# Activation rows 288 floats apart and weight slots on multiples of 256 bytes in a three-block transformer kernel

## The chip, the cores and the metric

The kernel is one launch on one NeuronCore of a Trainium2 chip. The metric is the device time of one execution in microseconds, median of the runs. All arithmetic is float32; the results are [1, 256, 1024] float32.

## What is computed

Three layers on 256 tokens of width 1024. The first two carry 16 meta tokens as well, 272 in all.

```python
def swiglu(x, w_gate, w_up, w_down):
    return (jax.nn.silu(x @ w_gate) * (x @ w_up)) @ w_down

h = concat(meta_tokens, x)                       # 272 tokens
for i in range(2):
    h = h + 0.5 * rmsnorm(swiglu(rmsnorm(h, g0), ...), g1)     # d_ff 2816
    m = neighborhood_attention(...) if i == 0 else diff_attention(...)
    h = h + rmsnorm(m, g3)
    h = h + 0.5 * rmsnorm(swiglu(rmsnorm(h, g4), ...), g5)
x = h[16:]                                       # 256 tokens
x = x + rms_norm(mix(rms_norm(x)) @ w_out, g)    # block attention and mLSTM
x = x + rms_norm(square(relu(rms_norm(x) @ w_up)) @ w_down, g) # width 4096
```

From the last attention's output on (sub-layer 4), only the 256 tokens are carried.

## The kernel before, in words

The work is eight sub-layers (`SUBS`, numbered k = 0 to 7): four FFNs (0, 2, 3, 5), three mixers (NA = 1, DA = 4, MIX = 6) and the last MLP (7). Each has two phases (`PHASES[2k]`, `PHASES[2k+1]`): a product from the normalised input x, and a product from the hidden or attended activations back to the residual h. Activations are held transposed, features on the 128 partitions and tokens along a row: `x_hi[:, k, :]` is chunk k of 8, one row per partition.

**Three products.** Each float32 operand is split in a high and a low part of type float32r. `product` (lines 645 to 648) issues `w_hi` x `x_hi` (L646), `w_hi` x `x_lo` (L647) and `w_lo` x `x_hi` (L648) for one chunk k and one half m of a panel; `chunk` does both halves, so one row k of the activations is read by six matmuls in a row: hi, lo, hi, hi, lo, hi. The weights are the stationary operand (128 x 128 floats), the activations the moving one, with 272 or 256 columns. `shared_chunk` (L709, L715) does the same for the first two panels of a sub-layer together, 96 matmuls in each of eight openings; `opening_panel` (L733) is the very first panel, 48 matmuls. `row_products` (L874 to L876), in the last phase, swaps the operands: `mlp_hi`/`mlp_lo` are stationary and 512 columns of `w_hi`/`w_lo` move.

**Panels.** A panel is 256 output columns by up to 1024 rows of weights, 8192 bytes a partition. SP loads it into one of four slots of `raw` (L534) in pieces of 1024 bytes, ScalarE rounds it to `w_hi` (L1400), VectorE subtracts to `w_lo` (L1856), in place over `raw`. A chunk takes 1024 bytes of a slot, its half m 512.

**Second phase of an FFN.** VectorE draws gate and up from the accumulators (`z`, L1999), ScalarE applies silu, VectorE multiplies (L2663), ScalarE rounds to `hid_hi` (L1828) and VectorE writes the rest to `hid_lo` (L2666), two of the 22 rows at a time. `down` then reads `hid_hi[:, k, :]` and `hid_lo[:, k, :]` as moving rows.

**Order.** Each engine runs a program written out by hand, tied by semaphores; no planner decides it.

**Addresses.** A program-wide cursor places all buffers in SBUF by hand (`sb`), every one on a multiple of 64 bytes. `region` and what follows is used in turn by the sub-layers. The first free byte is 16481, and so the buffers of this change start here (bytes in a partition; row k is 272 x 4 = 1088 bytes on, 64 modulo 256):

| buffer | start | modulo 256 | rows start, modulo 256 |
|---|---|---|---|
| w_lo (and raw) | 16512 | 128 | every chunk and half 128 |
| w_hi | 49280 | 128 | every chunk and half 128 |
| x_hi | 90752 | 128 | 128, 192, 0, 64, and again |
| x_lo | 99456 | 128 | the same |
| hid_hi | 140608 | 64 | 64, 128, 192, 0 |
| hid_lo | 164544 | 192 | 192, 0, 64, 128 |
| mlp_hi, mlp_lo | 140608, 173376 | 64 | all 64 (rows of 1024 bytes) |

Of the kernel before, what the change touches and what calls it, by code (L numbers as in the profile page):

```python
# [22 lines left out]
F32 = mybir.dt.float32  # L23
# [7 lines left out]
NM = 16  # L31
NT = NX + NM
FF = 2816
FC = FF // P
# [101 lines left out]
def program(nc, A, out):  # L136

    with ExitStack() as ctx:
# [3 lines left out]

        start = (nc.sbuf_base + 63) // 64 * 64
        cursor = [start]
# [12 lines left out]
        x_hi_at = cursor[0]  # L157
        x_hi = sb("x_hi", [P, DC, NT], F32R)
        x_lo_at = cursor[0]
        x_lo = sb("x_lo", [P, DC, NT], F32R)  # L160
        y_at = cursor[0]
# [22 lines left out]
        root = sb("root", [P, 4, 8])  # L184
        region = cursor[0]
        bias_at = region + 2 * FC * NT * 4
        end = bias_at + 32 * NT * 4
# [3 lines left out]
        c = [region]  # L191
        hid_hi = sb("hid_hi", [P, FC, NT], F32R, c)
        hid_lo = sb("hid_lo", [P, FC, NT], F32R, c)

# [40 lines left out]
        assert c[0] <= z_at  # L235
        c = [end]
        line = sb("line", [8, 2 * NT - 1 - NM], F32, c)
        assert c[0] <= nc.sbuf_usable_end

# [232 lines left out]
        def out_bank(k, g):  # L472

            return acc[:, :, g % 2, :] if k == NA else acc[:, g % 2, :, :]
# [169 lines left out]
        def _(pe):  # L644
# [75 lines left out]
            def opening_panel():  # L720

                for part, xs, ready in ((w_hi, x_hi, x_hi_ready), (w_hi, x_lo, x_ready), (w_lo, x_hi, None)):
                    if part is w_lo:
                        pe.wait_ge(w_lo_ready, 1)
                    for k in range(DC):
                        if ready is not None:
                            pe.wait_ge(ready, k + 1)
                        if ready is x_hi_ready and k == 0:
                            keep_warm(aux[:, 3, :], 12)
                            pe.wait_ge(w_hi_ready, 1)  # L730
                        for m in range(2):
                            w = slice(k * CW + m * P, k * CW + m * P + P)
                            mm = nc.tensor.matmul(acc[:, 0, m, 0:NT], part[:, 0, w], xs[:, k, :],  # L733
                                                  start=ready is x_hi_ready and k == 0,
                                                  stop=part is w_lo and k == DC - 1)
                mm.then_inc(panel_used, 1)
# [83 lines left out]
            def from_na_heads():  # L820
# [6 lines left out]
                for c in range(8):  # L827
                    if c in (2, 3):
                        na_turn(2 * c)
                        na_turn(2 * c + 1)  # L830
                    pe.wait_ge(x_ready, SPLIT_HEADS[NA] + c + 1)
                    mm = chunk(out_bank(NA, 0)[:, :, 0:NT], slot, c, x_hi, x_lo, c, c == 0, c == 7)
                mm.then_inc(panel_used, 1)
# [554 lines left out]
        def _(act):  # L1388
# [343 lines left out]
            for k in range(8):  # L1732
# [3 lines left out]
                if k in (NA, DA, MIX):  # L1736
# [32 lines left out]
                    if k == NA:  # L1769
# [6 lines left out]
                        for c in range(8):  # L1776
                            if c == 2:
                                high(n, 2, 5)
                            act.wait_ge(s["o_turned"], c + 1)
                            nc.scalar.activation(x_hi[:, c, :], na_banks[c][:, 0:NT], ACT.Copy).then_inc(x_hi_ready, 1)  # L1780
                        act.wait_ge(lam_step, 2)
# [64 lines left out]
        def _(dve):  # L1846
# [598 lines left out]
            for k in range(8):  # L2445
# [3 lines left out]
                if k in (NA, DA, MIX):  # L2449
# [50 lines left out]
                    if k == NA:  # L2500
# [41 lines left out]
                        for c in range(8):  # L2542
                            if c == 4:
                                evict_rows(k, 8)
                            if c in (0, 4):
                                dve.wait_ge(meta_gathered, 28 + c)
                            dve.wait_ge(x_hi_ready, SPLIT_HEADS[k] + c + 1)
                            nc.vector.tensor_tensor(x_lo[:, c, :], na_banks[c][:, 0:NT], x_hi[:, c, :].bitcast(F32),
                                                    ALU.subtract).then_inc(x_ready, 1)
# [268 lines left out]
```

## Time and profile before

| | |
|---|---|
| median of 3 runs | 1434.66 us (1434.41 to 1439.29) |
| profiled execution, span from first to last instruction | 1436.0 us |
| PE (TensorE matmul) busy | 1419.0 us, 99%, 10988 matmuls |
| DVE (VectorE) busy | 947.8 us, 66% |
| ACT (ScalarE) busy | 662.0 us, 46% |
| POOL (GpSimd) busy | 45.6 us, 3% |
| chain that ended last | PE 92%, DVE 3%, ACT 2%, DMA 2% |
| granted TensorE clock, mean | 0.998 |

The times of the runs are those of whole executions; the profiled execution's own time is known by its span only, and that is 1.3 us over the median. Matmuls overlap, so a matmul's duration in the rows (0.28 us) is not what it costs: cost is the distance from its start to the next one's. A stretch of the trace with n matmuls in it gives that distance as its length over n.

### The profile page before, as it was taken

To read this page: it belongs to the slowest core of one execution; us is meant where nothing else is said; L and a number is where in the kernel's file an instruction comes from. 1 tells how busy PE (TensorE), PEld (TensorE's weight loads), DVE (VectorE), ACT (ScalarE), POOL (GpSimd) and SP (SyncE) were. 2 spreads that over 40 slices of the span, in tenths; PEclk is the share of its full clock that TensorE was granted. 3 is DMA by queue.
4 is the path that set the end of the run, shared out by engine and by line. 5 is a ranking of instruction groups with operands and counts; after the bars stand their busy time and mean duration, and the time that the engine had idled before them with its cause. 6 is when DMAs were issued, how large, how long until landed. Compare 5 with 4: busy or idle time off the path is not lost.

```text
span 1436.0 us, 26258 instructions
## 1 busy us (share of the span) xinstructions
PE 1419.0 (99%) x10988; PEld 1361.9 (95%) x10988; DVE 947.8 (66%) x1223; ACT 662.0 (46%) x876; POOL 45.6 (3%) x72
## 2 busy tenths in 40 slices
PE   9999999999999999999999999999999999999998
PEld 9999999978999999999999988999999997999887
DVE  6656568566865555866557677876656975787653
ACT  5444345544544343544435357544444555544432
POOL 0000010010000000000001000000001010000000
PEclk9999999999999999999999999999999999999999
DMA  7586765511455576455454640465656540356552
GB/s 219 177 226 186 206 195 161 176 61 60 147 176 175 173 217 200 147 176 175 145 168 157 205 147 2 146 206 176 191 175 205 172 152 30 119 176 208 187 195 99
DMA packets 238904, 233.99 MB, mean 163 GB/s; under 512 B 29791, under 2 KB 233492, under 8 KB 238816
## 3 DMA queue, kind: packets, MB, share of 16 engines
q1 hardware_dynamic: 238024, 232.33, 52.4%
q8 instruction: 66, 1.08, 0.3%
q10 hardware_dynamic: 792, 0.40, 0.1%
q14 instruction: 22, 0.18, 0.0%
HBM read 231.52 MB, written 1.12 MB: 162 GB/s over the span
## 4 chain that ended last, share of the span: by engine, by line
PE 92%; DVE 3%; ACT 2%; DMA 2%; issue 1%; DVEq 0%; SPq 0%; ACTq 0%
PE acc L646 22%; PE acc L647 22%; PE acc L648 22%; PE acc L709 4%; PE aux L876 2%; PE aux L875 2%; PE aux L874 2%; PE acc L715 2%; PE aux L646 2%; PE aux L647 2%; PE aux L648 2%; PE aux L941 1%; PE acc L1154 1%; ACT w_hi L1400 1%; PE acc L1262 1%
## 5 line engine op out<-in xcount | busy, mean ns | idle before, releaser
L646 PE MATMUL acc<-x_hi,w_hi 128*128 128x272 f32 (+1 forms) x1960 | 559.8, 286 | 1.6 <-DVE z L1999 0.9
L647 PE MATMUL acc<-x_lo,w_hi 128*128 128x272 f32 (+1 forms) x1960 | 559.6, 286 | 0.0
L1856 DVE TENSOR_TENSOR w_lo<-raw,w_hi 128x2048 fp32r<-128x2048 f32 (+1 forms) x229 | 482.0, 2109 | 117.3 <-ACT w_hi L1400 116.6
L648 PE MATMUL acc<-x_hi,w_lo 128*128 128x272 f32 (+1 forms) x1960 | 557.9, 285 | 0.0
L1400 ACT ACTIVATE w_hi<-raw 128x2048 fp32r<-128x2048 f32 (+3 forms) x251 | 407.0, 1627 | 171.1 <-DMA raw<-in_ffn_w_down 52.7
L646 PEld LDWEIGHTS acc<-x_hi,w_hi 128*128 128x128 f32 x1960 | 369.4, 188 | 4.5 <-issue 1.7
L647 PEld LDWEIGHTS acc<-x_lo,w_hi 128*128 128x128 f32 x1960 | 368.2, 188 | 0.3 <-issue 0.2
L648 PEld LDWEIGHTS acc<-x_hi,w_lo 128*128 128x128 f32 x1960 | 368.3, 188 | 0.0
L646 PE MATMUL acc<-hid_hi,w_hi 128*128 128x272 f32 (+1 forms) x704 | 201.9, 287 | 0.0
L647 PE MATMUL acc<-hid_lo,w_hi 128*128 128x272 f32 (+1 forms) x704 | 201.6, 286 | 0.0
L648 PE MATMUL acc<-hid_hi,w_lo 128*128 128x272 f32 (+1 forms) x704 | 200.7, 285 | 0.0
L1999 DVE TENSOR_TENSOR z<-acc,rstd 128x544 f32<-128x544 f32 (+1 forms) x95 | 67.2, 712 | 136.0 <-PE acc L648 135.8
L1828 ACT ACTIVATE hid_hi<-z 128x544 f32 (+3 forms) x44 | 28.7, 652 | 248.5 <-DVE z L2663 246.4
L648 PEld LDWEIGHTS acc<-hid_hi,w_lo 128*128 128x128 f32 x704 | 132.6, 188 | 0.0
L647 PEld LDWEIGHTS acc<-hid_lo,w_hi 128*128 128x128 f32 x704 | 132.6, 188 | 0.0
L646 PEld LDWEIGHTS acc<-hid_hi,w_hi 128*128 128x128 f32 x704 | 132.4, 188 | 0.1
L709 PE MATMUL acc<-x_hi,w_hi 128*128 128x272 f32 (+1 forms) x256 | 66.2, 289 | 4.7 <-ACT x_hi L1463 4.7
L709 PE MATMUL acc<-x_hi,w_lo 128*128 128x272 f32 (+1 forms) x256 | 64.9, 284 | 0.0
L646 PE MATMUL aux<-x_hi,w_hi 128*128 128x272 f32 (+1 forms) x200 | 59.0, 295 | 1.9 <-DVE w_lo L1856 1.9
L2666 DVE TENSOR_TENSOR hid_lo<-z,hid_hi 128x544 f32 (+3 forms) x44 | 31.6, 718 | 40.3 <-ACT hid_hi L1828 40.3
L647 PE MATMUL aux<-x_lo,w_hi 128*128 128x272 f32 (+1 forms) x200 | 57.7, 288 | 0.0
L648 PE MATMUL aux<-x_hi,w_lo 128*128 128x272 f32 (+1 forms) x200 | 57.6, 288 | 0.0
(340 smaller groups left out, 1610.5 us busy)
## 6 DMA issues: line engine op xcount, KB each, us to landing
raw<-in_ffn_w_gate SPq DMA_DIRECT2D x44, 1024.0 KB, 5.4
raw<-in_ffn_w_up SPq DMA_DIRECT2D x44, 1024.0 KB, 5.4
raw<-in_ffn_w_down SPq DMA_DIRECT2D x32, 768.0 KB, 4.9
raw<-in_ffn_w_down SPq DMA_DIRECT2D x32, 640.0 KB, 4.4
raw<-in_w_up SPq DMA_DIRECT2D x16, 1024.0 KB, 5.4
raw<-in_w_down SPq DMA_DIRECT2D x16, 1024.0 KB, 4.8
raw<-in_na_w_qkv SPq DMA_DIRECT2D x12, 1024.0 KB, 5.2
raw<-in_da_w_qkv SPq DMA_DIRECT2D x12, 1024.0 KB, 5.3
```

The source lines that it names most:

```text
L646: nc.tensor.matmul(o, wh, xh, start=first, stop=False)
L647: nc.tensor.matmul(o, wh, xl, start=False, stop=False)
L648: return nc.tensor.matmul(o, wl, xh, start=False, stop=last)
L709: nc.tensor.matmul(banks(n, 0, j)[:, m, 0:tokens], part[:, (ph.p0 + j) % SLOTS, w], x_hi[:, k, 0:tokens], start=k == 0 and part is w_hi, s ...
L715: mm = nc.tensor.matmul(banks(n, 0, j)[:, m, 0:tokens], w_hi[:, (ph.p0 + j) % SLOTS, w], x_lo[:, k, 0:tokens], start=False, stop=k == DC - 1)
L874: nc.tensor.matmul(o, mlp_hi[:, k, tok], w_hi[:, slot, w], start=first, stop=False)
L875: nc.tensor.matmul(o, mlp_hi[:, k, tok], w_lo[:, slot, w], start=False, stop=False)
L876: return nc.tensor.matmul(o, mlp_lo[:, k, tok], w_hi[:, slot, w], start=False, stop=last)
L1400: ins = nc.scalar.activation(w_hi[:, slot, w], raw[:, slot, w], ACT.Copy)
L1856: nc.vector.tensor_tensor(w_lo[:, slot, w], raw[:, slot, w], w_hi[:, slot, w].bitcast(F32), ALU.subtract)\
L1999: ins = nc.vector.tensor_tensor(dst, src, spread(0, tokens), ALU.mult)
L2666: nc.vector.tensor_tensor(hid_lo[:, dst, 0:tokens], up, hid_hi[:, dst, 0:tokens].bitcast(F32), ALU.subtract).then_inc(hid_ready, 1)
```

## The change

Constants and addresses. A new `STRIDE = 288` replaces 272 as the row length of `x_hi`, `x_lo`, `hid_hi` and `hid_lo`; the 16 floats at a row's end are not used, and the code that took whole rows now takes `0:NT`. A row is 1152 bytes, 128 modulo 256. The cursor starts at a multiple of 256 bytes, and so does `region`. The constant `line`, which had its own place at the end, moves to `y_at`. The buffers then start at 16640 (w_lo), 49408 (w_hi), 90880 (x_hi), 100096 (x_lo), 141824 (hid_hi), 167168 (hid_lo), 141824 and 174592 (mlp_hi, mlp_lo), all 0 modulo 256; the rows of x and hid start at 0 and 128 modulo 256 in turn, the weight chunks and the mlp rows all at 0. Buffers behind them move along.

No instruction is added, removed or moved on any engine, and no wait changes. Only the form of those that write `hid_hi` and `hid_lo` is another: two rows of 272 (2 x 272) where there were 544 floats in one piece.

```diff
--- before.py
+++ after.py
@@ -30,6 +30,7 @@
 NX = 256
 NM = 16
 NT = NX + NM
+STRIDE = 288
 FF = 2816
 FC = FF // P
 FF2 = 4096
@@ -140,7 +141,7 @@
             return ctx.enter_context(nc.semaphore(name))
 
 
-        start = (nc.sbuf_base + 63) // 64 * 64
+        start = (nc.sbuf_base + 255) // 256 * 256
         cursor = [start]
 
         def sb(name, shape, dt=F32, at=None):
@@ -155,9 +156,9 @@
         w_hi = sb("w_hi", [P, SLOTS, FULL * CW], F32R)
         h = sb("h", [P, DC, NT])
         x_hi_at = cursor[0]
-        x_hi = sb("x_hi", [P, DC, NT], F32R)
+        x_hi = sb("x_hi", [P, DC, STRIDE], F32R)
         x_lo_at = cursor[0]
-        x_lo = sb("x_lo", [P, DC, NT], F32R)
+        x_lo = sb("x_lo", [P, DC, STRIDE], F32R)
         y_at = cursor[0]
         y = sb("y", [P, DC, NT])
         z = sb("z", [P, 2, 2, 2, NT])
@@ -182,15 +183,15 @@
         stat = sb("stat", [P, 4, 16])
         na_mask = sb("na_mask", [P, GRID_W])
         root = sb("root", [P, 4, 8])
-        region = cursor[0]
-        bias_at = region + 2 * FC * NT * 4
+        region = (cursor[0] + 255) // 256 * 256
+        bias_at = region + 2 * FC * STRIDE * 4
         end = bias_at + 32 * NT * 4
         assert end <= nc.sbuf_usable_end, (end, nc.sbuf_usable_end)
 
 
         c = [region]
-        hid_hi = sb("hid_hi", [P, FC, NT], F32R, c)
-        hid_lo = sb("hid_lo", [P, FC, NT], F32R, c)
+        hid_hi = sb("hid_hi", [P, FC, STRIDE], F32R, c)
+        hid_lo = sb("hid_lo", [P, FC, STRIDE], F32R, c)
 
         c = [region]
         mlp_hi = sb("mlp_hi", [P, FF2 // P, NX], F32R, c)
@@ -233,9 +234,8 @@
         meta_in = sb("meta_in", [16, NM], F32, c)
         bands = sb("bands", [16, BANDS], F32, c)
         assert c[0] <= z_at
-        c = [end]
+        c = [y_at]
         line = sb("line", [8, 2 * NT - 1 - NM], F32, c)
-        assert c[0] <= nc.sbuf_usable_end
 
         c = [region]
         proj = sb("proj", [P, 24, NT], F32, c)
@@ -730,7 +730,7 @@
                             pe.wait_ge(w_hi_ready, 1)
                         for m in range(2):
                             w = slice(k * CW + m * P, k * CW + m * P + P)
-                            mm = nc.tensor.matmul(acc[:, 0, m, 0:NT], part[:, 0, w], xs[:, k, :],
+                            mm = nc.tensor.matmul(acc[:, 0, m, 0:NT], part[:, 0, w], xs[:, k, 0:NT],
                                                   start=ready is x_hi_ready and k == 0,
                                                   stop=part is w_lo and k == DC - 1)
                 mm.then_inc(panel_used, 1)
@@ -829,7 +829,8 @@
                         na_turn(2 * c)
                         na_turn(2 * c + 1)
                     pe.wait_ge(x_ready, SPLIT_HEADS[NA] + c + 1)
-                    mm = chunk(out_bank(NA, 0)[:, :, 0:NT], slot, c, x_hi, x_lo, c, c == 0, c == 7)
+                    mm = chunk(out_bank(NA, 0)[:, :, 0:NT], slot, c, x_hi[:, :, 0:NT], x_lo[:, :, 0:NT], c,
+                               c == 0, c == 7)
                 mm.then_inc(panel_used, 1)
                 for j in (1, 2):
                     panel(n, 0, j, ph.a0 + j - 1, out_bank(NA, j), range(8), True, True, x_hi[:, :, 0:NT], x_lo[:, :, 0:NT],
@@ -1777,7 +1778,7 @@
                             if c == 2:
                                 high(n, 2, 5)
                             act.wait_ge(s["o_turned"], c + 1)
-                            nc.scalar.activation(x_hi[:, c, :], na_banks[c][:, 0:NT], ACT.Copy).then_inc(x_hi_ready, 1)
+                            nc.scalar.activation(x_hi[:, c, 0:NT], na_banks[c][:, 0:NT], ACT.Copy).then_inc(x_hi_ready, 1)
                         act.wait_ge(lam_step, 2)
                         nc.scalar.activation(lam[:, 2:4], lam[:, 0:2], ACT.Exp).then_inc(lam_exp, 1)
                     if k == DA:
@@ -2545,7 +2546,7 @@
                             if c in (0, 4):
                                 dve.wait_ge(meta_gathered, 28 + c)
                             dve.wait_ge(x_hi_ready, SPLIT_HEADS[k] + c + 1)
-                            nc.vector.tensor_tensor(x_lo[:, c, :], na_banks[c][:, 0:NT], x_hi[:, c, :].bitcast(F32),
+                            nc.vector.tensor_tensor(x_lo[:, c, 0:NT], na_banks[c][:, 0:NT], x_hi[:, c, 0:NT].bitcast(F32),
                                                     ALU.subtract).then_inc(x_ready, 1)
 
                         dve.wait_ge(lam_exp, 1)
```

## Rows read from the trace of the kernel before

**Rows 1.** Five stretches: length, busy us (count) per engine PE to POOL, clock, DMA.

```profile
395.00:495.00 100.00, 100.00 (x802) 100.00 (x801) 60.99 (x51) 41.78 (x35) 0.00 (x0) 1.00 0.57 177
505.00:560.00 55.00, 55.00 (x442) 55.00 (x441) 30.95 (x26) 22.34 (x20) 4.64 (x3) 1.00 0.69 201
...
945.00:1040.00 95.00, 95.00 (x815) 95.00 (x814) 61.58 (x53) 42.73 (x36) 0.00 (x0) 1.00 0.58 180
1045.00:1095.00 50.00, 50.00 (x425) 50.00 (x424) 28.91 (x27) 21.98 (x20) 5.65 (x6) 1.00 0.58 184
...
1345.00:1420.00 75.00, 75.00 (x329) 61.56 (x328) 36.98 (x21) 27.33 (x16) 0.00 (x0) 1.00 0.50 175
```

**Rows 2.** Groups by shape, PE: line, names, shape, count, busy us, mean ns.

```profile
L647 PE MATMUL acc<-x_lo,w_hi 128*128 128x272 f32 x1248 | 360.9, 289 | 0.0
...
L646 PE MATMUL acc<-x_hi,w_hi 128*128 128x256 f32 x712 | 200.7, 282 | 1.5 <-DVE z L1999 0.9 <-DVE x_lo L2189 0.6
...
L646 PE MATMUL acc<-hid_hi,w_hi 128*128 128x272 f32 x528 | 152.3, 288 | 0.0
...
L646 PE MATMUL acc<-hid_hi,w_hi 128*128 128x256 f32 x176 | 49.6, 282 | 0.0
...
L646 PE MATMUL aux<-x_hi,w_hi 128*128 128x272 f32 x112 | 32.9, 294 | 0.0
...
L646 PE MATMUL aux<-x_hi,w_hi 128*128 128x256 f32 x88 | 26.1, 297 | 1.9 <-DVE w_lo L1856 1.9
```

**Rows 3.** Timeline of PE, first matmul of rows k = 4 to 7 and 0, 272 columns.

```profile
604.51 0.28 PE L646 MATMUL acc<-x_hi,w_hi 128*128 128x272 f32 x1
...
605.27 0.28 PE L646 MATMUL acc<-x_hi,w_hi 128*128 128x272 f32 x1
...
606.02 0.29 PE L646 MATMUL acc<-x_hi,w_hi 128*128 128x272 f32 x1
...
606.77 0.28 PE L646 MATMUL acc<-x_hi,w_hi 128*128 128x272 f32 x1
...
607.51 0.28 PE L646 MATMUL acc<-x_hi,w_hi 128*128 128x272 f32 x1
```

**Rows 4.** Timeline of PE, the same five places in a half panel with 256 columns.

```profile
972.58 0.28 PE L646 MATMUL acc<-x_hi,w_hi 128*128 128x256 f32 x1
...
973.29 0.28 PE L646 MATMUL acc<-x_hi,w_hi 128*128 128x256 f32 x1
...
974.00 0.28 PE L646 MATMUL acc<-x_hi,w_hi 128*128 128x256 f32 x1
...
974.70 0.28 PE L646 MATMUL acc<-x_hi,w_hi 128*128 128x256 f32 x1
...
975.39 0.28 PE L646 MATMUL acc<-x_hi,w_hi 128*128 128x256 f32 x1
```

**Rows 5.** Timeline of PE, first matmul of rows 8, 9 and 10 of hid, 256 columns.

```profile
1048.44 0.28 PE L646 MATMUL acc<-hid_hi,w_hi 128*128 128x256 f32 x1
...
1049.14 0.29 PE L646 MATMUL acc<-hid_hi,w_hi 128*128 128x256 f32 x1
...
1049.86 0.28 PE L646 MATMUL acc<-hid_hi,w_hi 128*128 128x256 f32 x1
```

**Rows 6.** Timeline of PE, runs of matmuls whose weight load sets the distance.

```profile
217.12 1.95 PE L941 MATMUL aux<-ones 128*128 128x128 f32 x16
...
334.04 1.90 PE L1154 MATMUL acc<-v_rows,turned_pair 128*128 128x64 f32 x16
```

**Rows 7.** Groups by shape, DVE: eviction of z and writing of hid_lo.

```profile
L1999 DVE TENSOR_TENSOR z<-acc,rstd 128x544 f32<-128x544 f32 x61 | 43.9, 724 | 103.4 <-PE acc L648 103.3
...
L2666 DVE TENSOR_TENSOR hid_lo<-z,hid_hi 128x544 f32 x24 | 17.4, 726 | 22.9 <-ACT hid_hi L1828 22.9
```

**Rows 8.** Waits of PE; chain of waits: start us, us, what.

```profile
PE acc L709 <- ACT x_hi L1463: 4.7, 7, 1.3
...
559.88 7.11 DMA raw<-in_ffn_w_up
```

## The prediction, made before the changed kernel ran

> **What bounds the kernel now.** I read the busy time of every engine in five long stretches first, then the instruction groups by shape, then the timeline of TensorE inside single panels, and last the waits and the chain of waits. In the five stretches [rows 1] TensorE is busy the whole time (100.00 of 100.00 us), at the full granted clock (1.00, its 2.4 GHz level), while VectorE has 61 and ScalarE 42 us of work in 100. So inside a phase nothing but the spacing of the matmuls counts. The spacing comes from the counts: 802 matmuls touch the stretch 395 to 495, about 2 of them begun before it, so 100 us / 800 = 125.0 ns for one with 272 columns of x. In the same way 505 to 560 gives 125.1 (272 columns of hid), 945 to 1040 gives 116.9 (256, x), 1045 to 1095 gives 118.3 (256, hid) and 1345 to 1420 gives 229.1 (512 columns).
>
> How many there are: the shapes [rows 2] show one of the three lines of a product, so each count stands three times. 272 columns of x: 3 x (1248 + 112) = 4080, and 48 of the opening panel and 384 of the shared openings (eight openings of 96 matmuls, four of them with 272 columns): 4512. 272 of hid: 3 x 528 = 1584. 256 of x: 3 x (712 + 88) + 384 = 2784. 256 of hid: 3 x 176 = 528. With the spacings above that is 564 + 198 + 325 + 62 = 1149 us of a span of 1436.0; 384 matmuls of 512 columns add 88. A nanosecond on each of the 9408 is 9.4 us, or 0.66%, and that is the lever of this change.
>
> **Does the address of a row show in the trace?** It does. All weight chunks start at 128 modulo 256 bytes; rows of x start at 128, 192, 0, 64 in turn. In one half panel of 272 columns [rows 3] the four blocks of six matmuls, one block for each row k, take 0.76, 0.75, 0.75 and 0.74 us. With 256 columns [rows 4] they take 0.71, 0.71, 0.70 and 0.69 us. Such half panels repeat, in steps of 3.00 and 2.81 us, through the whole phase. In hid with 256 columns [rows 5] the block of row 8 (hi at 64, lo at 192) takes 0.70 us and that of row 9 (hi at 128, lo at 0) 0.72 us. Three times the same sign: rows on a multiple of 128 bytes are not the cheap ones. They average (0.76 + 0.75) / 12 = 125.8 ns against 124.2 with 272 columns, (0.71 + 0.70) / 12 = 117.5 against 116.7 with 256.
>
> **Part by part.**
> Moving rows, 288 floats apart. Rows now start at 0 and 128 in turn, in x and in hid, so only two of the four classes are left, and both stand in the trace before. 272 columns of x: 125.8 is read from starts with 10 ns steps, a nanosecond is its error, and against 125.0 it is +0.8; the neighbouring reading, all four blocks alike, is 0; I take +0.6, nearer to the one that shows a difference: 4512 x 0.6 ns = +2.7 us. 272 of hid: to the same 125.6 from 125.1, 1584 x 0.5 = +0.8 us. 256 of x: 117.5 against the mean of rows 4, 2.81 / 24 = 117.1, 2784 x 0.4 = +1.1 us. 256 of hid: today hi and lo lie 128 bytes apart in phase, and afterwards they are alike as in x, so from 118.3 to 117.5: 528 x -0.8 = -0.4 us. Sum +4.2 us.
>
> Weights at 0 modulo 256 instead of 128. No row shows the slots elsewhere. The nearest are matmuls with few columns, whose spacing is that of their weight load: sixteen with the stationary tile ones (at 192) span 1.95 us, sixteen with v_rows (at 64) 1.90 us [rows 6]; less the last one's own 0.28, and over fifteen, that is 0.11 for both. The start of the load makes no difference there, so I take 0 for it alone. Its phase relative to the moving row is another matter: rows of x lie at 0, 64, 128, 192 beyond the weights now and at 0 and 128 afterwards, which are the same two blocks that I used. Phase by itself and phase against the weights give the same sum; only an effect of both together would break it. Bounds for moving rows and weights as one: every block like the cheapest (0.74 / 6 = 123.3 and 0.69 / 6 = 115.0) is -1.7 x 6096 - 2.1 x 2784 - 3.3 x 528 = -18.0 us; every block like the dearest (0.76 / 6 = 126.7, 0.72 / 6 = 120.0) is +1.7 x 6096 + 2.9 x 2784 + 1.7 x 528 = +19.3 us. Farther down lies the price of a column in the 512-column matmuls, 229.1 / 512 = 0.447 ns, where starts count half as much: 121.7 and 114.5 ns, -29 us. The 384 matmuls of 512 columns move too (0 instead of 128 under w, 0 instead of 64 under the stationary mlp tiles): at most 2 ns each either way, 0.8 us, taken as 0.
>
> The Trainium skill (SBUF — State Buffer, section on the DMA port swizzle) says that SBUF is read in 16-byte lines, and by that alone all four classes would cost the same and the change would do nothing. Rows 3 to 5 do not agree: 0.69 and 0.71 us for the same six shapes. The skill (TensorE: Matmul & The Clock Gate, Part 2) also says that loading the next weights takes no read bandwidth from the running matmul; by that rule the phase between the two is nothing, and the sum stays at the 4.2 us from the rows alone.
>
> VectorE and ScalarE forms. The 44 pairs that write hid go from 544 contiguous floats to 2 x 272. hid_lo takes 726 ns today; the eviction of z from two accumulator banks, whose source is already in two pieces, takes 724 [rows 7]. Nothing to pay, and both engines have a third of the time free [rows 1]: if it cost 50 ns, it would hide under a panel of 6 us. The order of instructions and all waits are unchanged on every engine, SP's queue included. The table line lies over onehot, which the matmul that precedes it has read: nothing.
>
> DMA. Weights now land on multiples of 256. The longest transfer on the chain takes 7.11 us ahead of a sub-layer's opening; TensorE waits there for x_hi, 4.7 us over seven openings [rows 8]. Those 4.7 us bound any gain; a loss has no reason. I take 0, since the chain passes VectorE and ScalarE work after the landing. The skill (DMA: Bandwidth & Descriptors, How a descriptor splits into AXI transactions) lets each of our 1 KB pieces fall from 36 beats to 32, if it holds for the writing side, which no row here shows.
>
> **Sum.** 1434.7 + 4.2 = 1438.9 us. The sum was made on the profiled execution, whose span of 1436.0 is 1.3 us above the median of the runs, 1434.7; I add it to the median.
>
> **Rivals.**
> Faster: with both operands on multiples of 128 the stalls vanish, as they nearly do today in the block at 64 (0.69 us). For it: 125.0 and 116.9 ns both lie above columns alone (272 at 0.447 = 121.7, 256 at 0.447 = 114.5), the excess varies with the address, and hid with mixed phases is dearer than x (118.3 against 116.9). Against it: the blocks at 0 and 128 are the slow ones. All blocks at the cheapest: 1434.7 - 18.0 = 1417.
> Slower: moving row and weights start on the same phase in even rows and collide. Even rows pay the dearest block (126.7 and 120.0), odd rows stay at today's mean. +0.85 x 6096 + 1.45 x 2784 + 0.1 x 528 = +9.3 us: 1444. It decides from 0.8 ns a matmul (7.2 us) on. For it: the block at 128, in phase with its weights, is the longest of rows 3. Against: in rows 4 the one at 192 is as long.
> No effect: the block differences come from what stands before a matmul and average out in any layout: 1434.7. Here too if the phase matters within 64 bytes only, since every start stays a multiple of 64.
>
> **Chances.** Forecast 0.36, no effect 0.12, faster rival 0.30, slower rival 0.22. A measurement of this kernel can tell about 0.5% (7.2 us) from no change. Of the forecast's case 0.01 falls to faster and 0.04 to slower, so faster 0.31, same 0.43, slower 0.26. The range reaches from 1414, past the cheapest blocks, to 1447, past the slower rival, and leaves out about 0.2: the 29 us case and the dearest blocks everywhere.
>
> **What would show it.** Right: matmul counts in stretches of the same phase and length of about 798 instead of 802 (100 us, 272 columns of x), about 812 instead of 815 (95 us, 256 of x), about 428 instead of 425 (50 us, 256 of hid); blocks of two kinds only, taking turns. Wrong: a spacing under 124 or 116 ns, or over 126.5; a change of wait times at the openings by more than 2 us; hid_lo over 800 ns.

## The result, and the profile after

| | median | range | runs |
|---|---|---|---|
| before | 1437.14 us | 1434.41 to 1439.72 | 6 |
| changed | 1442.89 us | 1441.04 to 1444.94 | 6 |

The ratio is 1.0044, interval 1.0025 to 1.0062. The change costs 5.75 us by the medians and 6.1 us by the profiled spans (1442.1 against 1436.0). That is a small, real loss, and under the 0.5% that the prediction set as its bound for "slower". In some executions of either kernel the granted clock falls to its 1.2 GHz level for a few microseconds and the runs of one kernel lie some 5 us apart, so it helps to compare those with a mean clock of 1.000: 1434.4 to 1435.2 us for the kernel before (four of 17 in the last series below), 1441.0 and 1442.8 for the changed one.

Line numbers behind L800 are one higher in the changed kernel. These are its five stretches, answering to [rows 1] (columns as there; each kind of stretch begins some microseconds later than before):

```profile
395.00:495.00 100.00, 100.00 (x797) 99.90 (x796) 60.97 (x53) 41.82 (x35) 0.00 (x0) 1.00 0.55 171
505.00:560.00 55.00, 55.00 (x440) 55.00 (x440) 31.41 (x28) 21.88 (x20) 4.63 (x3) 1.00 0.69 196
945.00:1040.00 95.00, 95.00 (x805) 95.00 (x804) 60.15 (x51) 41.52 (x35) 0.00 (x0) 1.00 0.59 185
1050.00:1100.00 50.00, 50.00 (x425) 50.00 (x424) 29.61 (x26) 21.35 (x19) 7.27 (x8) 1.00 0.59 180
1352.00:1427.00 75.00, 75.00 (x333) 62.12 (x332) 36.93 (x21) 27.34 (x16) 0.00 (x0) 1.00 0.51 174
```

TensorE is still busy throughout at full clock, so again the counts are the spacing. They are 797 for 802 (272 columns of x), 440 for 442 (272 of hid), 805 for 815 (256 of x), 425 for 425 (256 of hid) and 333 for 329 (512 columns). Three kinds got slower, one stayed, one got faster. The prediction's signs were 798, 812 and 428 for x with 272 and 256 columns and hid with 256: the first came true, the other two did not.

For finer numbers I took the distance from the start of one matmul to the start of the one hundreds later, inside one long phase, divided by their number (816 or 552 matmuls of x, 498 of hid). "First" is the opening FFN, "later" are the two others with 272 columns. All values in ns:

| | before | after |
|---|---|---|
| 272, x, first / later | 125.0 / 125.0 | 126.1 / 125.6 |
| 272, hid, first / later | 125.5 / 125.1 | 126.3 / 125.6 |
| 256, x | 116.9 | 118.3 |
| 256, hid | 118.4 | 118.3 |
| 512 | 229.1 | 227.0 |

The timeline of TensorE in the changed kernel, 272 columns, first matmul of five successive rows k (start us, duration us; answers to [rows 3]):

```profile
613.10 0.29 PE L646 MATMUL acc<-x_hi,w_hi 128*128 128x272 f32 x1
...
613.85 0.29 PE L646 MATMUL acc<-x_hi,w_hi 128*128 128x272 f32 x1
...
614.61 0.29 PE L646 MATMUL acc<-x_hi,w_hi 128*128 128x272 f32 x1
...
615.36 0.29 PE L646 MATMUL acc<-x_hi,w_hi 128*128 128x272 f32 x1
...
616.12 0.29 PE L646 MATMUL acc<-x_hi,w_hi 128*128 128x272 f32 x1
```

The blocks take 0.75, 0.76, 0.75 and 0.76 us (748, 759, 747 and 759 ns by the starts in the trace): two kinds taking turns, as forecast. Those in phase with the weights are the cheaper ones. The same with 256 columns, answering to [rows 4]:

```profile
949.50 0.28 PE L646 MATMUL acc<-x_hi,w_hi 128*128 128x256 f32 x1
...
950.22 0.28 PE L646 MATMUL acc<-x_hi,w_hi 128*128 128x256 f32 x1
...
950.93 0.28 PE L646 MATMUL acc<-x_hi,w_hi 128*128 128x256 f32 x1
...
951.64 0.28 PE L646 MATMUL acc<-x_hi,w_hi 128*128 128x256 f32 x1
...
952.35 0.28 PE L646 MATMUL acc<-x_hi,w_hi 128*128 128x256 f32 x1
```

0.72, 0.71, 0.71 and 0.71 us (713, 712, 707 and 708 ns), where the prediction took 0.705 (117.5 x 6). Here the two kinds do not take turns: rows k = 0 and 2 both start in phase with the weights, and are 6 ns apart. The two blocks at 0 and 128 cost more in this company than they did among the four.

**Where the 6.1 us lie.** Both kernels issue the same 10988 matmuls in the same order, so the start of matmul number n in one trace less that in the other shows where time is gained or lost. Over the three long phases with 272 columns of x: +0.9, +0.5 and +0.5 us. Over the three with 272 of hid: +0.4, +0.2, +0.2. Over the two long ones with 256 of x: +1.1 and +0.8. 256 of hid: 0.0. 512 columns: -0.8. That is +3.8 us from spacing. The first 150 matmuls give +1.0. Both kernels start 6 to 7 matmuls per microsecond at first and 11 later; the step comes before 5 us in the kernel before and before 7 us in the changed one, and the clock column, 1.00 throughout, does not tell why. The experiments scatter there from 0.0 to +1.2, and one and the same kernel (starts only, profiled twice) has +0.8 and 0.0, so no layout is charged with it. The mixer of sub-layer 6 gives +3.1, that of sub-layer 4 -1.1; what is left, the openings, the first mixer and short pieces, gives -0.7. The +3.1 is mostly a stretch at the lower clock that the profiled execution of before did not have. Windows of the changed kernel:

```profile
1200.00:1205.00 5.00, 4.55 (x30) 3.63 (x28) 3.12 (x11) 2.46 (x12) 0.00 (x0) 1.00 0.00 0
1205.00:1212.00 7.00, 7.00 (x25) 5.36 (x23) 3.85 (x10) 2.18 (x8) 0.00 (x0) 0.51 0.00 0
```

and of the kernel before:

```profile
900.00:906.00 6.00, 5.07 (x30) 5.07 (x31) 4.65 (x6) 3.53 (x3) 1.91 (x1) 0.72 0.98 319
1205.00:1212.00 7.00, 6.96 (x44) 5.32 (x44) 3.58 (x13) 4.25 (x19) 0.00 (x0) 1.00 0.01 2
```

The clock column is 0.51 there (1.2 GHz) against 1.00 (2.4 GHz), while TensorE had been busy 4.55 of the 5 us ahead of it. The profile before has such a piece in sub-layer 4's mixer instead (0.72 over 900 to 906), the changed kernel has none there. Such pieces come and go between executions (of the two profiles of starts only, one has such a piece of 3.4 us and the other none) and are no part of the change's own cost.

Little else moved. The wait lists of TensorE name L709 for x_hi with 4.5 us over seven openings (4.7 in [rows 8]). VectorE's groups by shape, answering to [rows 7]:

```profile
L2000 DVE TENSOR_TENSOR z<-acc,rstd 128x544 f32<-128x544 f32 x61 | 43.9, 724 | 105.4 <-PE acc L648 105.3
L2667 DVE TENSOR_TENSOR hid_lo<-z,hid_hi 128x544 f32 x24 | 17.4, 726 | 22.9 <-ACT hid_hi L1829 22.9
```

hid_lo in two pieces of 272 takes the same 726 ns as in one of 544. The long transfer of the chain, answering to the 7.11 us of [rows 8]:

```profile
563.26 6.37 DMA raw<-in_ffn_w_up
```

It takes 0.7 us less, and the stretch ahead of the opening of sub-layer 3, which waits for it, shrinks from 5.9 to 5.2 us. The weights' start is not the reason: in the two profiles of starts only (below), with weights at 0, the stretch takes 5.9 and 6.3 us, and in the layout with weights at 128 and x at 0 it takes 5.0. It has 5.9 us or more in every profile with rows of x 272 floats apart, and 5.2 or less in every one with longer rows. Why is open.

### The profile page after: what moved, and what is told of

Read it like the earlier page. It is cut to its first block, busy times and chain, and to the rows that moved or that the text cites. A ratio compares the mean times of both kernels' runs of the same rounds, so it can differ in the third digit from the quotient of the medians.

```text
span 1442.1 us, 26258 instructions
## 1 busy us (share of the span) xinstructions
PE 1426.3 (99%) x10988; PEld 1370.1 (95%) x10988; DVE 947.4 (66%) x1223; ACT 661.7 (46%) x876; POOL 45.5 (3%) x72
## 4 chain that ended last, share of the span: by engine, by line
PE 93%; DVE 3%; ACT 2%; DMA 1%; issue 1%; DVEq 0%; SPq 0%; ACTq 0%
PE acc L646 22%; PE acc L647 22%; PE acc L648 22%; PE acc L709 4%; PE aux L877 2%; PE aux L875 2%; PE aux L876 2%; PE acc L715 2%; PE aux L646 2%; PE aux L647 2%; PE aux L648 2%; PE aux L942 1%; PE acc L1155 1%; ACT w_hi L1401 1%; PE acc L1263 1%
## 5 line engine op out<-in xcount | busy, mean ns | idle before, releaser
L709 PE MATMUL acc<-x_hi,w_hi 128*128 128x272 f32 (+1 forms) x256 | 66.6, 290 | 4.5 <-ACT x_hi L1464 4.5
L709 PE MATMUL acc<-x_hi,w_lo 128*128 128x272 f32 (+1 forms) x256 | 65.2, 285 | 0.0
```

The lines of the kernel that those rows point to most:

```text
L709: nc.tensor.matmul(banks(n, 0, j)[:, m, 0:tokens], part[:, (ph.p0 + j) % SLOTS, w], x_hi[:, k, 0:tokens], start=k == 0 and part is w_hi, s ...
```

## Experiments

**Theory.** The spacing is set by where the moving row starts relative to the stationary tile, modulo 256 bytes ("beyond the weights"), not by the row's own address. **Rivals:** the row's own address counts; or only the mixture of phases counts; or one of the two parts of the change (rows apart, buffers' start) carries the whole loss. In the first four expectations, theory P is the distance, theory M the row's own address, rival T a cost of the row length or of a changing phase.

All experiments write `X_ROW` and `HID_ROW` where the changed kernel has `STRIDE`. The first four give every row of x the same phase (320 floats, 1280 bytes, are a multiple of 256), leave hid at 272 floats and at its old distance from the weights, and place the weights and x. Diffs are against the changed kernel, and "..." stands for lines left out.

### All rows of x 192 bytes beyond the weights, two ways

```diff
-STRIDE = 288
+X_ROW = 320
+HID_ROW = 272
...
-        start = (nc.sbuf_base + 255) // 256 * 256
+        start = (nc.sbuf_base + 127) // 256 * 256 + 128
...
         h = sb("h", [P, DC, NT])
+        cursor[0] = (cursor[0] + 191) // 256 * 256 + 64
         x_hi_at = cursor[0]
...
-        region = (cursor[0] + 255) // 256 * 256
+        region = (cursor[0] + 191) // 256 * 256 + 64
```

> Rows of x 320 floats (1280 bytes, a multiple of 256) apart, so that all 16 rows start at 64 modulo 256, weights at 128 as before the change, hid as before (272 apart). Theory P (phase of the moving row against the weight chunk sets the spacing): the cheapest block of before for all rows, 115.3 ns with 256 columns and 123.6 ns with 272, so about -11 us on the span of before (1436). Theory M (the moving row's own phase, whatever the weights): the same here. Rival T (what costs is the change of phase from row to row, or the row stride itself): same spacing in all kernels with this stride. Rival N (blocks differ by accident): 125.0 and 117.0, as before.

The second has the same distance at another address: weights at 0, x and region at 192.

```diff
         start = (nc.sbuf_base + 255) // 256 * 256
...
+        cursor[0] = (cursor[0] + 63) // 256 * 256 + 192
         x_hi_at = cursor[0]
...
-        region = (cursor[0] + 255) // 256 * 256
+        region = (cursor[0] + 63) // 256 * 256 + 192
```

> The same, but everything moved: weights at 0, all rows of x at 192, so 192 beyond the weights as in one_phase_64, and hid in the same place relative to the weights. Theory P: spacings equal to one_phase_64 within 0.3 ns. Theory M: those of rows at 192 in before, 125.1 ns with 272 columns and 117.8 with 256, about 2 ns more than one_phase_64.

### All rows 128 beyond, and in phase

As the first, but with x at 0, `cursor[0] = (cursor[0] + 255) // 256 * 256`, and with x at 128, `cursor[0] = (cursor[0] + 127) // 256 * 256 + 128`. The weights are at 128 in both.

> All rows of x at 0, weights at 128 (128 apart). Theory P and M: the blocks of before at 0, 125.8 ns with 272 columns, 117.0 with 256; P says also 126.5 for 272 from the odd rows of the changed kernel, which stand 128 from their weights too. Rival T: equal to one_phase_64.

> All rows of x at 128, in phase with the weights. Theory P: between the blocks of before at 128 (125.4 and 117.9 ns) and the even rows of the changed kernel (125.0 and 118.2). Theory M: 126.5 with 272 columns, as the rows at 128 in the changed kernel. Rival T: equal to one_phase_64.

The four together: 1425.84, 1425.88, 1446.86 and 1453.8 us, one run each, against 1439.8 for the kernel before in the same series. Windows of the kernel before, 272 and 256 columns of x:

```profile
400.00:490.00 90.00, 90.00 (x722) 90.00 (x721) 54.03 (x45) 38.56 (x31) 0.00 (x0) 1.00 0.57 175
950.00:1030.00 80.00, 80.00 (x686) 80.00 (x685) 51.25 (x43) 35.89 (x29) 0.00 (x0) 1.00 0.61 191
```

x at 64, weights at 128 (the third row is in the last MLP, 256 columns too):

```profile
400.00:490.00 90.00, 90.00 (x732) 90.00 (x732) 55.65 (x46) 36.25 (x29) 0.00 (x0) 1.00 0.58 181
950.00:1030.00 80.00, 80.00 (x682) 80.00 (x681) 49.82 (x44) 34.83 (x29) 0.00 (x0) 1.00 0.59 182
1292.00:1322.00 30.00, 30.00 (x268) 30.00 (x266) 23.03 (x23) 13.24 (x11) 0.00 (x0) 1.00 0.66 209
```

x at 192, weights at 0:

```profile
400.00:490.00 90.00, 90.00 (x732) 90.00 (x731) 55.66 (x46) 36.60 (x30) 0.00 (x0) 1.00 0.58 180
950.00:1030.00 80.00, 80.00 (x708) 80.00 (x708) 50.75 (x44) 34.65 (x29) 0.00 (x0) 1.00 0.61 191
1292.00:1322.00 30.00, 30.00 (x257) 30.00 (x256) 22.60 (x22) 12.20 (x10) 0.00 (x0) 1.00 0.67 212
```

x at 0, weights at 128:

```profile
400.00:490.00 90.00, 90.00 (x713) 90.00 (x712) 55.09 (x47) 37.38 (x31) 0.00 (x0) 1.00 0.55 173
950.00:1030.00 80.00, 80.00 (x676) 80.00 (x675) 51.34 (x43) 34.06 (x28) 0.00 (x0) 1.00 0.58 181
```

x and weights both at 128; the first row is the opening FFN:

```profile
52.00:142.00 90.00, 90.00 (x713) 90.00 (x712) 53.44 (x45) 34.59 (x28) 0.00 (x0) 1.00 0.70 197
400.00:490.00 90.00, 90.00 (x721) 90.00 (x720) 54.74 (x47) 39.37 (x32) 0.00 (x0) 1.00 0.55 174
950.00:1030.00 80.00, 80.00 (x669) 80.00 (x669) 49.56 (x43) 34.70 (x29) 0.00 (x0) 1.00 0.58 184
```

With 272 columns, the two layouts at 192 beyond give the same 90 us / 730 = 123.3 ns, and 128 beyond gives 90 / 711 = 126.6. The one at 0 differs from the one at 64 in nothing but 64 bytes of start, and its three long phases with 272 columns take 8.0 us more; all 4512 matmuls at 3.3 ns would be 15 us, an estimate. In phase gives 126.6 in the first FFN and 125.2 later. Rival T is out, as four layouts of one row length differ. The distance holds as theory P has it, but P's numbers, read off the blocks of the mixture, often missed: 128 beyond with 256 columns took 118.7 and not 117.0, in phase took 120.0 and not 118. The last layout also sat at the lower clock for 20.5 us in the mixer of sub-layer 6, which cost it 9.5 us there, so its time of 1453.8 overstates it.

With 256 columns a second thing shows. The two layouts of the same distance take turns: 80 / 680 = 117.6 and 30 / 266 = 112.8 in one, 80 / 706 = 113.3 and 30 / 255 = 117.6 in the other. By starts over whole phases these are 117.78 and 113.33 ns in both. One distance has two steady spacings here, and what decides between them was not found. With 256 columns the distance thus fixes the spacing only up to this choice.

### The same row address, other weights

Weights at 128 and x at 192, 64 beyond.

```diff
-        start = (nc.sbuf_base + 255) // 256 * 256
+        start = (nc.sbuf_base + 127) // 256 * 256 + 128
...
+        cursor[0] = (cursor[0] + 63) // 256 * 256 + 192
         x_hi_at = cursor[0]
...
-        region = (cursor[0] + 255) // 256 * 256
+        region = (cursor[0] + 191) // 256 * 256 + 64
```

> All rows of x at 192, weights at 128: the phase that is missing, 64 beyond the weights (one_phase_192 had 192 beyond). Theory P: the settled part of before's blocks at 192, 117.5 with 256 columns, 125.1 with 272. If only odd multiples of 64 mattered, it would equal one_phase_64: 123.3.

1442.72 us (before: 1439.46 in this series). Windows:

```profile
400.00:490.00 90.00, 90.00 (x713) 90.00 (x712) 55.08 (x47) 37.69 (x32) 0.00 (x0) 1.00 0.55 171
950.00:1030.00 80.00, 80.00 (x708) 80.00 (x708) 54.02 (x47) 37.11 (x32) 0.00 (x0) 1.00 0.59 185
1292.00:1322.00 30.00, 30.00 (x257) 30.00 (x256) 22.67 (x22) 12.19 (x10) 0.00 (x0) 1.00 0.62 191
```

Rows of x at 192 as in the second experiment, but 713 matmuls in 90 us instead of 732: 126.6 for 123.3 ns. Here only the weights' start differs, and with it the phase between the two (and the start of region, which x's products with 272 columns do not touch). This is the comparison that decides against the rival of the row's own address. With 256 columns, 64 beyond has the same two spacings as 192 beyond, 113.3 and 117.8. Both numbers of the expectation, 125.1 and 117.5, missed: the row's price alone isn't that of its block in the mixture.

VectorE, ScalarE and the DMA queues write the weight slots, so their addresses moved with the weights too. Do they set the spacing? In the first experiment I sorted some 600 matmuls of sub-layer 2 (272 columns) by what ran beside them. They are 123.3 ns apart where VectorE works all the time (354) and where it pauses (206), 123.3 where ScalarE works (238) and where it pauses (330), and 123.3 where no DMA engine moves data (197). With x at 0 each of these groups has 126.7. So the 3.3 ns aren't a matter of the other engines; TensorE's own two streams, weights and moving rows, are left.

### The two parts of the change alone

Starts only: rows 272 floats apart as before, everything else as the changed kernel.

```diff
-STRIDE = 288
+X_ROW = 272
+HID_ROW = 272
```

> The second part of the change alone: weights, x_hi, x_lo and region start at 0 modulo 256, rows stay 272 floats apart. Theory P (phase of the moving row against the weight chunk): the rows of x stand 0, 64, 128, 192 from the weights as in before, in hid the four phases only begin elsewhere; spacings as in before within 0.2 ns (125.0 and 117.0, hid 125.1 and 118.4), span within 1 us of before's. Rival A (alignment of the weights to 256 counts by itself): another spacing everywhere.

Rows only: 288 floats apart, starts as before (weights and x at 128, region at 64).

```diff
-STRIDE = 288
+X_ROW = 288
+HID_ROW = 288
...
-        start = (nc.sbuf_base + 255) // 256 * 256
+        start = (nc.sbuf_base + 127) // 256 * 256 + 128
...
-        region = (cursor[0] + 255) // 256 * 256
+        region = (cursor[0] + 191) // 256 * 256 + 64
```

> The first part alone: rows of x and hid 288 floats apart, starts as in before (weights at 128, x at 128, region at 64). Theory P: x stands 0 and 128 from its weights in turn, as in the changed kernel: 125.6 and 118.3 ns. hid_hi and hid_lo stand at 192 and 64 from them: between one_phase_64's 123.3 and the unseen phase 64, so below 125.0 with 272 columns and below 118 with 256. Sum: 2 to 4 us under the changed kernel. Rival A: the loss comes with the starts, and this kernel is no slower than before in x.

Starts only took 1434.82 us, and was timed again in more rounds:

> starts_only again, timed: starts at 0 modulo 256, rows 272 apart. Theory P: ratio 0.9985 to 1.001 against before; only the last phase gains, 384 matmuls of 512 columns at 2.1 ns, 0.8 us. Rival A (the starts carry a part of the change's +5.7 us): 1.001 or more.

1436.71 us against 1437.93, ratio 0.9996, interval 0.9985 to 1.0007: the starts alone are worth nothing that can be measured. (The first profile's span, 1433.0 against 1436.0, is shorter than the 1 us of the expectation allows, for it has no stretch at the lower clock; the second has 1434.8.) Windows of starts only, 272 and 256 columns of x:

```profile
400.00:490.00 90.00, 90.00 (x722) 90.00 (x721) 54.11 (x45) 39.37 (x32) 0.00 (x0) 1.00 0.56 175
950.00:1030.00 80.00, 80.00 (x686) 80.00 (x686) 49.68 (x43) 34.36 (x29) 0.00 (x0) 1.00 0.61 189
...
1342.00:1417.00 75.00, 75.00 (x333) 62.10 (x332) 37.84 (x22) 27.37 (x16) 0.00 (x0) 1.00 0.52 179
```

The counts of the split matmuls are those of the kernel before, 722 and 686. Moving weights and rows of x together leaves every distance between them as it was, and every spacing with it, which is the theory once more. (hid meets the same four distances, begun at another one.) Only the 512 columns gain (333 for 329), all that the change had to offer.

Rows only took 1448.24 us (before: 1439.46):

```profile
400.00:490.00 90.00, 90.00 (x719) 90.00 (x719) 55.81 (x47) 39.12 (x32) 0.00 (x0) 1.00 0.55 173
950.00:1030.00 80.00, 80.00 (x679) 80.00 (x678) 51.23 (x43) 35.64 (x30) 0.00 (x0) 1.00 0.60 186
...
1050.00:1090.00 40.00, 40.00 (x347) 40.00 (x346) 22.93 (x20) 15.43 (x14) 1.30 (x1) 1.00 0.62 192
```

In x it has the whole loss: 126.11, 125.56 and 118.33 ns by starts, to the hundredth those of the changed kernel. Its hid, 64 and 192 beyond the weights in turn instead of 0 and 128, goes the other way, to 116.1 ns with 256 columns. The time of 1448.24 holds 20.5 us at the lower clock, in this profile:

```profile
1205.00:1212.00 7.00, 7.00 (x26) 5.58 (x25) 3.68 (x9) 2.44 (x11) 0.00 (x0) 0.50 0.01 2
1212.00:1225.00 13.00, 13.00 (x55) 10.09 (x54) 4.50 (x25) 5.22 (x21) 0.00 (x0) 0.60 0.00 0
```

That mixer is 8.9 us longer than before; the rest of the kernel only 1.5, of which 1.2 lie in the first 150 matmuls. By the times alone one would have charged all of it to the rows. The expected 2 to 4 us under the changed kernel therefore did not show in the span (1446.4 against 1442.1). Of its spacings, that of hid with 256 columns came as expected, and 272 columns of hid took 125.0, which is the mean of 123.3 and 126.7, the prices of 192 and 64 beyond alone.

### Distances of 32 bytes

Is it the multiple of 64 bytes that matters? As the first experiment with x at 96 (224 beyond) and at 32 (160 beyond).

```diff
+        cursor[0] = (cursor[0] + 159) // 256 * 256 + 96
         x_hi_at = cursor[0]
```

> All rows of x at 96, weights at 128: 224 beyond the weights, a multiple of 32 bytes but not of 64. If 64-byte pieces are what is fetched, every row now touches one more piece: slower than both neighbours (123.3 at 192 beyond, 125.3 to 126.7 at 0), 2 to 3 ns above. If pieces are 32 bytes or less: between the neighbours, 124 to 125 ns.

```diff
+        cursor[0] = (cursor[0] + 223) // 256 * 256 + 32
         x_hi_at = cursor[0]
```

> All rows of x at 32, weights at 128: 160 beyond, between the cheapest phase seen (192 beyond, 123.3 ns with 272 columns) and a dear one (128 beyond, 126.7). If the cost goes with the distance between the two streams: 125 ns, between them. If starts that are odd multiples of 32 pay an extra piece: 126.7 or more, as at 224 beyond.

1444.9 us (before 1439.46) and 1431.88 us (before 1437.93). All distances, by starts over whole phases, in ns:

| beyond the weights | 272, first / later FFNs | 256, FFN / last MLP |
|---|---|---|
| 0 | 126.67 / 125.33 | 120.00 / 120.00 |
| 64 | 126.67 / 126.67 | 113.33 / 117.78 |
| 128 | 126.67 / 126.67 | 118.67 / 118.66 |
| 160 | 123.33 / 123.33 | 118.66 / 117.32 |
| 192, x at 64 | 123.33 / 123.33 | 117.78 / 113.33 |
| 192, x at 192 | 123.33 / 123.33 | 113.33 / 117.78 |
| 224 | 126.67 / 126.67 and 125.33 | 118.33 / 118.34 |
| mixed, before | 125.00 / 125.00 | 116.94 / 116.95 |
| 0 and 128 in turn, after | 126.11 / 125.56 | 118.33 / 118.33 |

No expectation came true here: with 272 columns 224 beyond (126.7, once 125.3) is no dearer than its neighbour in phase, and 160 beyond is as cheap as 192. Neither extra pieces at odd multiples of 32 nor a slow change with the distance describes the table. The good region with 272 columns holds 160 and 192 but neither 128 nor 224, so the effect is finer than 64 bytes. It isn't the same for both widths: 64 beyond is bad with 272 columns and can be the best with 256.

The Trainium skill (SBUF — State Buffer, section on the DMA port swizzle) has SBUF read in 16-byte lines. All these starts are multiples of 32, so by that rule alone the table would have one value in each column, and the runs do not agree.

### A layout that uses it

Rows of x 192 beyond everywhere, and hid 288 floats apart from 64, so that its rows lie 192 and 64 beyond in turn. To make room, y begins in the unused end of x_lo's last row.

```diff
-STRIDE = 288
+X_ROW = 320
+HID_ROW = 288
...
-        start = (nc.sbuf_base + 255) // 256 * 256
+        start = (nc.sbuf_base + 127) // 256 * 256 + 128
...
         h = sb("h", [P, DC, NT])
+        cursor[0] = (cursor[0] + 191) // 256 * 256 + 64
         x_hi_at = cursor[0]
...
+        x_lo = sb("x_lo", [P, DC, X_ROW], F32R)
+        cursor[0] -= 192
         y_at = cursor[0]
...
-        region = (cursor[0] + 255) // 256 * 256
+        region = (cursor[0] + 191) // 256 * 256 + 64
```

> The best of both: rows of x 320 floats apart, all 192 beyond the weights as in one_phase_64, and rows of hid 288 apart at 192 and 64 beyond in turn as in rows_only. From the spacings seen so far: x 123.3 ns with 272 columns and 113.3 to 117.8 with 256, hid 125.0 and 116.1. Against one_phase_64 (1425.8) hid gives 528 x 2.3 + 1584 x 0.1 = 1.4 us more, so 1424 to 1425; against before's median 0.992. Rival T (stalls find another place, e.g. in loads of weights, once the matmuls are faster): not under 1430.

1423.79 us (1419.63 to 1425.41, 6 runs) against 1437.93 (1434.12 to 1439.5, 17 runs): ratio 0.9906, interval 0.9888 to 0.9924. It beats both kernels, by 0.9% and, against the changed one's own median, by 1.3%. Windows, with hid's 256 columns last:

```profile
400.00:490.00 90.00, 90.00 (x732) 90.00 (x732) 55.32 (x46) 36.05 (x30) 0.00 (x0) 1.00 0.58 180
950.00:1030.00 80.00, 80.00 (x709) 80.00 (x708) 51.49 (x43) 35.46 (x30) 0.00 (x0) 1.00 0.61 192
1292.00:1322.00 30.00, 30.00 (x267) 30.00 (x266) 22.50 (x24) 13.67 (x12) 0.00 (x0) 1.00 0.64 212
1050.00:1090.00 40.00, 40.00 (x347) 40.00 (x346) 23.17 (x20) 15.05 (x13) 7.91 (x9) 1.00 0.64 199
```

Both long stretches with 256 columns of x are in the fast one of their two spacings (113.3), and hid stands at 40 us / 345 = 116 ns. The window of 272 columns is that of the first experiment. The time is the expected one, in part by luck. Against the first experiment's profile hid gave its 1.4 us as summed, and sub-layer 5's 256 columns of x gave 4.2 more by falling into the fast spacing, while the mixer of sub-layer 6, with a stretch at the lower clock, took 2.6 back. Not tried: all rows of hid at one phase (two buffers of 22 x 320 floats find no room), and weight chunks 1088 bytes apart, so that their phase follows rows of 272.

## Why the prediction was right, and where its steps were wrong

**Direction and size.** Forecast 1439.0, with +4.2 us over the kernel before; measured 1442.89 and +5.75. The likeliest case came true, inside the half per cent. Part of the gap in the absolute number is the base. The profiled execution of the changed kernel took 1443.88 us at a span of 1442.1, so 1.8 us lie outside the span. The profile before, with 1436.0, was thus a run of about 1437.8, some 3 us over the 1434.7 that the sum was added to and not 1.3; three runs did not show that the middle of more is 1437.1.

**How much of it is luck.** The long phases give +3.8 us of spacing and the openings +0.5, near the forecast +4.2, but by errors that offset each other: 256 columns of x cost more than forecast and 256 of hid gave nothing back, while 512 columns, put at nothing, gave 0.8 back. Of the 6.1 us between the two profiles, the +1.0 at the start and most of the +2.0 in the two mixers, where the clock differs, aren't the addresses' doing. The interval of the runs, 3.6 to 8.9 us, holds the forecast and cannot tell it from the 5.75.

**What bounds the kernel: right.** TensorE is busy in every window of the long phases, in every experiment, and the times follow the spacings.

**272 columns of x, +0.6 ns: right** for the later FFNs (+0.56); the first one took +1.1. The two kinds of block take turns with 272 columns; with 256 they do not.

**272 of hid, +0.5: right** (+0.4 later, +0.8 first).

**256 of x, +0.4 ns: mis-sized.** It measured +1.4 (118.33 against 116.94). At 2784 matmuls the term would be +3.9 us instead of +1.1. In the long phases alone it is +1.9. The step that failed is the one that read the price of a phase from its block among blocks of other phases. The sentence "phase by itself and phase against the weights give the same sum; only an effect of both together would break it" named the gap, but the break came from elsewhere: a block's cost depends on the layout around it. Alone, 192 beyond costs 123.3 ns with 272 columns, and the mean of the one-phase layouts at 0, 64, 128 and 192 (125.3 to 126.7, 126.7, 126.7, 123.3) is at least 125.5, where the mixture of the four measures 125.0. In turn, 0 and 128 beyond cost 118.3 with 256 columns, and alone 120.0 and 118.7. The cheapest block was read rightly: it is the one at 64, 192 beyond, in [rows 3] and [rows 4], and 0.74 / 6 = 123.3 ns is its price alone too. The blocks at 64 and 128 beyond stand at 0.75 / 6 = 125.0 in [rows 3] and cost 126.7 alone; the 0.70 / 6 = 116.7 of 128 beyond in [rows 4] is 118.7 alone.

**256 of hid, -0.8 ns: wrong** (-0.1). The reasoning that hid would become like x holds (118.34 and 118.33), but x itself was 0.8 dearer than taken. The third of the "three times the same sign" was a thin one: rows 8 and 9 of [rows 5] take 701 and 718 ns by the starts in the trace, but rows 12 and 13, with the same addresses modulo 256, take 709 and 710.

**Openings: right in kind.** The sum counted their 768 matmuls at full price, and they do pay: 96 matmuls take 12.11 us for 12.07 to 12.09 with 272 columns and 11.47 for 11.33 to 11.37 with 256, some +0.5 us over all eight. That the short pieces that hold them still came out 0.7 us shorter lies ahead of them: the stretches before the openings of sub-layers 3 and 6 shrank by 0.8 and 0.6 us. The second does so with starts only too, whose spacings are those of before; the first goes with the transfer shown above.

**512 columns, 0: within its bound, but not 0.** -2.1 ns each, -0.8 us, which is the 2 ns bound in full. The stationary tiles and the moving weights both start at 0 now, where the moving operand lay 64 beyond. That it is the distance again is supported by the second experiment, whose moving weights at 0 over mlp tiles at 192 are also 64 beyond, and stay at the 229 of before.

**VectorE's and ScalarE's form, waits, DMA: right, but for one transfer.** 726 ns as before, waits at the openings 4.5 for 4.7 us. DMA was put at nothing, and the longest transfer of the chain took 6.37 us for 7.11. The chain of waits has 93% TensorE, for 92%. The Trainium skill's rule that loading the next weights takes no read bandwidth from the running matmul (TensorE: Matmul & The Clock Gate, Part 2) would make the weights' start nothing. Rows of x at 192 with weights at 0 and at 128, 732 against 713 matmuls in 90 us, do not agree with it as far as the spacing goes. What inside the engine makes the distance count, no run here shows.

**The rivals.** "Faster" was wrong about the changed kernel, and its place was right: the lower spacings exist (123.3 and 113.3 ns), at 192 beyond and not at 0 and 128, and the size of its bound, -18 us, is near the -14 us that the best layout gave (in part by luck, as its bound has every phase at the cheapest block). "Slower", in phase as the dearest: 120.0 ns alone with 256 columns is indeed the dearest of the table and 126.7 with 272 shares that place, but between rows at 128 it isn't paid in full. "No effect" is excluded by the interval and by the counts; a phase that matters within 64 bytes only is excluded too, since 64-byte steps alone move 123.3 to 126.7.

## What to carry to other kernels

Where TensorE is busy end to end, divide the length of a stretch by its matmuls and compare layouts by that count, which shows differences well under 1% where single runs of one kernel lie 5 us apart. Place the moving operand by its distance from the stationary one modulo 256 bytes, with a row length that keeps that distance for all rows, and try the distances for each width: a round address is no good by itself (all starts at 0: nothing gained in the split matmuls; 192 beyond: 1%). Don't price a layout by reading one phase out of a mixture; run it with that phase alone.

## What was unexpected

- **Means in steps of eight cycles.** The one-phase spacings 113.33, 120.00, 123.33 and 126.67 ns are 272, 288, 296 and 304 cycles of the 2.4 GHz level; the others in the table lie between such values (118.33 is 284, 117.78 is 848 / 3). These are means: the single distances form a pattern that repeats. With 272 columns it is 122, 124, 123, 124, 122, 125 ns in the first experiment, six matmuls long, and 24 long with distances from 119 to 134 ns in the kernel before. Why the means fall on such steps, no run shows.
- **Two steady spacings in one layout.** 113.33 or 117.78 ns with 256 columns at 64 and 192 beyond, 125.33 or 126.67 with 272 columns in phase or 224 beyond, each kept through a whole phase of 816 or 552 matmuls. What picks one was not found; it is 4.4 ns of a matmul, 3.6 us in a phase of 816, so an edit elsewhere may move the time by as much. The first experiment and the last layout have the same starts of weights and x, and 117.78 and 113.33 ns in sub-layer 5.
- **The clock in the mixers.** In 12 of the 13 profiles the granted clock is at its 1.2 GHz level for 3.4 to 20.5 us in a mixer (sub-layer 4 or 6); in the changed kernel TensorE was busy 4.55 of the 5 us before. The longest of them made a mixer 9 us longer. It came with good and bad layouts alike.
